# Decay before the second query tile, recurrence between projections, xb to gd in three rounded passes, and a fill dealt out by TensorE's work

## What is computed

```python
z = rms_norm(x, norm_g) @ w_in      # w_in has 1024 rows; its columns are split into:
# qa ka va fa ga | xb gb | qc kcc vcc ksc vsc kwc vwc gate gc | ud vd gd | mg
y_a = fox_attention(rms_norm(qa), rms_norm(ka), va, fa + b_forget)   # adds a cumsum of log_sigmoid(fa)
y_b = rg_lru(conv4(xb), ...)        # two sigmoid gates, tanh/sqrt, a scan over the tokens
y_c = nsa_attention(rms_norm(qc), kcc, ..., vwc, sigmoid(gate))      # compressed + selected + window
y_d = gelu(ud) * (w_spatial @ layer_norm(gelu(vd)) + b_spatial)
ys = stack([y_a * silu(ga), y_b * silu(gb), y_c * silu(gc), y_d * silu(gd)])
merged = sum_n sigmoid(mg_n) * (ys_n @ w_branch_n)
x1 = x + merged @ w_out
```

## Time and profile before

| what | value |
| --- | --- |
| median of 3 runs | 1110.33 us (1109.07 to 1110.61) |
| the profiled execution, own time | 1109.99 us |
| span of its instructions | 1108.2 us |
| TensorE busy | 1005.1 us (91%) |
| VectorE busy | 611.6 us (55%) |
| ScalarE busy | 428.4 us (39%) |
| mean granted TensorE clock | 0.95 |

### The profile page before, as it was taken

How to read it: one execution, slowest core, us unless ns; L and a number is a source line. 1 busy time by engine, 2 the same in 40 slices (tenths; PEclk the granted TensorE clock), 3 DMA queues, 4 the chain that set the end, 5 groups by cost and what they waited for, 6 DMA issues and landing times.

```text
span 1108.2 us, 13860 instructions
## 1 busy us (share of the span) xinstructions
PE 1005.1 (91%) x5638; PEld 762.2 (69%) x5638; DVE 611.6 (55%) x1065; ACT 428.4 (39%) x699; POOL 48.2 (4%) x66
## 2 busy tenths in 40 slices
PE   7979999679997999989879999996889999999984
PEld 5767778446687989849867886896775753566521
DVE  4776521767364464416565599574852621587605
ACT  3345441283465363214365200435651400466401
POOL 1000000000000000000010123000000000000010
PEclk9989999799999999999989999998899999999986
DMA  9725776463424393356143124200898997999993
GB/s 301 227 82 189 262 267 227 152 228 134 171 77 166 111 351 129 116 183 204 36 143 110 44 76 152 77 1 34 323 354 294 352 377 287 399 405 405 408 349 125
DMA packets 110413, 230.66 MB, mean 208 GB/s; under 512 B 8300, under 2 KB 15757, under 8 KB 110350
## 3 DMA queue, kind: packets, MB, share of 16 engines
q1 hardware_dynamic: 104144, 216.44, 54.0%
q0 software_dynamic: 2880, 9.71, 2.3%
q10 hardware_dynamic: 3326, 3.63, 1.1%
HBM read 221.11 MB, written 8.65 MB: 207 GB/s over the span
## 4 chain that ended last, share of the span: by engine, by line
PE 70%; DVE 16%; DMA 6%; ACT 4%; issue 3%; ACTq 0%; DVEq 0%
PE bank L770 10%; PE bank L1510 6%; PE bank L1511 6%; PE bank L1512 6%; PE bank L2573 6%; PE bank L735 5%; PE bank L2512 4%; PE bank L2513 4%; PE bank L2514 4%; PE bank L2597 3%; DMA more_slots<-in_moe_w_up 2%; PE bank L2505 2%; PE bank L1424 1%; DMA slot<-in_ada_w 1%; PE bank L1553 1%
## 5 line engine op out<-in xcount | busy, mean ns | idle before, releaser
L1510 PE MATMUL bank<-rounded 128*128 128x256 f32 (+1 forms) x656 | 201.4, 307 | 14.6 <-DVE slot_rounded L659 8.7
L1511 PE MATMUL bank<-rounded 128*128 128x256 f32 x592 | 168.6, 285 | 0.0
L1510 PEld LDWEIGHTS bank<-rounded 128*128 128x128 f32 x656 | 126.4, 193 | 26.0 <-issue 17.0
L1512 PE MATMUL bank<-rounded,slot_rounded 128*128 128x256 f32 x472 | 135.0, 286 | 0.0
L770 PE MATMUL bank<-x_and_h,slot 128*128 128x256 f32 x544 | 127.5, 391 | 4.9 <-ACT x_and_h L574 4.9
L770 PEld LDWEIGHTS bank<-x_and_h,slot 128*128 128x128 f32 x544 | 104.9, 196 | 23.3 <-issue 8.9
L1511 PEld LDWEIGHTS bank<-rounded 128*128 128x128 f32 x592 | 114.5, 193 | 1.2 <-issue 1.0
L1500 DVE TENSOR_TENSOR slot_rounded<-slot,rounded 128x1024 fp32r<-128x1024 f32 (+1 forms) x63 | 67.1, 1086 | 67.7 <-ACT rounded L1494 67.5
L1512 PEld LDWEIGHTS bank<-rounded,slot_rounded 128*128 128x128 f32 x472 | 91.6, 194 | 0.0
L818 ACT ACTIVATE arena<-bank 128x256 f32<-128x256 f32 x56 | 21.5, 384 | 135.3 <-PE bank L770 108.6
L1494 ACT ACTIVATE rounded<-slot 128x1024 fp32r<-128x1024 f32 (+1 forms) x63 | 57.7, 943 | 27.1 <-PE bank L1512 23.3
(11 more groups left out here) (491 smaller groups left out, 2027.3 us busy)
## 6 DMA issues: line engine op xcount, KB each, us to landing
slot<-in_w_in SPq DMA_DIRECT2D x26, 2048.0 KB, 8.0
slot<-in_ada_w SPq DMA_DIRECT2D x12, 2048.0 KB, 8.2
slot<-in_moe_w_down SPq DMA_DIRECT2D x11, 2048.0 KB, 16.1
more_slots<-in_moe_w_gate SPq DMA_DIRECT2D x8, 2048.0 KB, 15.2
more_slots<-in_moe_w_up SPq DMA_DIRECT2D x8, 2048.0 KB, 17.9
slot<-in_moe_w_gate SPq DMA_DIRECT2D x7, 2048.0 KB, 10.0
x_and_h<-in_moe_w_up SPq DMA_DIRECT2D x6, 2048.0 KB, 15.3
more_slots<-in_moe_w_down SPq DMA_DIRECT2D x5, 2048.0 KB, 17.2
```

Of the source, the lines that this page charges most:

```text
L1510: t.do.matmul(dst, w_hi, x_hi, start=start, stop=False)
L1511: t.do.matmul(dst, w_hi, x_lo, start=False, stop=False)
L1512: return t.do.matmul(dst, w_lo, x_hi, start=False, stop=stop)
```

## The change

1. `decay` moves up in `PLAN`, between the two token tiles of qa. For it SyncE loads `sel` and the 8 columns of `w_f` ahead of the third weight (va), and GpSimd makes its three copies before its other constants.
2. xb (its last two of four channel jobs), gc, gb, ud, vd and gd become three-pass jobs: 18 `channels` jobs and 4 `pieces` jobs (which take the place of two `tokens` jobs of vd) join `FIRST_PIECES`, with 24 new homes. Their hidden-state parts come from `h1_split`, which moves up to stand behind the scores of the last fox unit. As before, the high part is made on ScalarE and the low part on VectorE.
3. `early`, `lru` and `spatial` are written in another order: xb first, then gc, gb and ud, with `conv`, `lru_gates` and `lru` one by one between them.
4. `woven(..., two_behind=24)` is replaced by two calls of `balanced`, which deals out the fill so that its work (by the table `WORK`) per attention job is even, once over the fox units and once over the sparse ones.

```diff
+def balanced(main, fill, cost):
+    whole = sum(cost.get(job[0], 0) for job in fill)
+    fill, out, put = deque(fill), [], 0
+    for n, job in enumerate(main):
+        out.append(job)
+        while fill and (put * len(main) < whole * (n + 1) or not cost.get(fill[0][0])):
+            put += cost.get(fill[0][0], 0)
+            out.append(fill.popleft())
+    return out + list(fill)
...
+        FIRST_HOMES += [M0, M1] + [Y3, M0, M1, SQ0] + [SQ1, Y3, SQ0, SQ1] + [Y3, SQ0, V_HOME, Y3] + [SQ0, V_HOME, Y3, SQ0] + [V_HOME, SQ0, M0, V_HOME]
...
+        LATER_FIRST = len(FIRST_PIECES)
+        FIRST_PIECES += [*channels("xb")[2:], *channels("gc"), *channels("gb"), *channels("ud"), *in_pieces("vd"), *channels("gd")]
+        def piece_beside(job):
+            if job in channels("xb", 2):
+                return LATER_FIRST + job[2]
+            p = FIRST_PIECES.index(job) + 2 if job in FIRST_PIECES else len(FIRST_PIECES)
+            return p if p not in (LATER_FIRST, LATER_FIRST + 1) and p < len(FIRST_PIECES) else None
...
-        PLAN = [..., ("first_start",), *tokens("qa"), FIRST_PIECES[0], ("head_norm", "qa"),
+        PLAN = [..., ("first_start",), ("tokens", "qa", 0), ("decay",), ("tokens", "qa", 1), FIRST_PIECES[0], ("head_norm", "qa"),
-                FIRST_PIECES[6], ("decay",), FIRST_PIECES[7], ("cond",), ...
+                FIRST_PIECES[6], FIRST_PIECES[7], ("cond",), ...
...
+        early += [("cmp_hidden", 0), ("cmp_hidden", 1), ("cmp_flip", 0), xs[0], ("cmp_flip", 1), ("cmp_out",), xs[1], ("conv", 0), ("cmp_keys",), xs[2], ("conv", 1),
+                  ("cmp_scores", 0), xs[3], ("conv", 2), ("cmp_scores", 1), ("cmp_turn", 0), gc[0], ("conv", 3), ("cmp_turn", 1)]
+        lru = [gc[1], ("lru_gates", 0, 0), ("lru_gates", 0, 1), ("softplus",), gc[2], ("lru_gates", 0, 2), ("lru_gates", 0, 3), gc[3], ("lru", 0),
+               ("lru_gates", 1, 0), ("lru_gates", 1, 1), gb[0], ("lru", 1), ("lru_gates", 1, 2), ("lru_gates", 1, 3), gb[1], ("lru", 2),
+               gb[2], ("lru", 3), gb[3], ("lru", 4), ud[0], ("lru", 5), ud[1], ("lru", 6)]
+        WORK = {"pieces": 47, "channels": 25, "tokens": 48, "gates": 19, ...}
+        spatial = [*ud[2:], *in_pieces("vd"), ("spatial_norm",), *channels("gd"), *[("spatial", j) for j in range(WT)]]
...
-        PLAN += woven(scored[:last_units], fill, 24)
+        PLAN += balanced(scored[:first_sparse], fill[:begun], WORK) + balanced(scored[first_sparse:last_units], fill[begun:], WORK)
-        PLAN.insert(PLAN.index(("ada", 6)), ("h1_split",))
+        PLAN.insert(PLAN.index(("scores", UNITS[2 * WT - 1])) + 1, ("h1_split",))
...
+        def sync_decay_constants(s):
+            s.do.dma_start(sel, d["sel"]).then_inc(*dma("sel_in"))
+            s.wait_ge(*at("w_f_clear"))
+            s.do.dma_start(w_f[:, :, 0:NH], w_in[:, :, COL["fa"]:COL["fa"] + NH]).then_inc(*dma("w_f_in"))
...
+                if n == 2:
+                    sync_decay_constants(s)
```

More of the change, by code:

```diff
@@ L413, in build @@
         early = [*kv, *qc[0:2], ("keys_norm", 0), qc[2], ("keys_norm", 1), qc[3], ("gates", 0), ("keys", 0), ("gates", 1), ("head_norm", "qc"),
[L414 to L419, removed]
+                 ("keys", 1), ("cmp_in", 0), ("heads", "qc", 0), ("heads", "qc", 1), ("cmp_in", 1), ("cmp_blocks",)]
+        xs, gc, gb, ud = channels("xb"), channels("gc"), channels("gb"), channels("ud")
+        early += [("cmp_hidden", 0), ("cmp_hidden", 1), ("cmp_flip", 0), xs[0], ("cmp_flip", 1), ("cmp_out",), xs[1], ("conv", 0), ("cmp_keys",), xs[2], ("conv", 1),
[3 more added lines that the diff above has]
+               gb[2], ("lru", 3), gb[3], ("lru", 4), ud[0], ("lru", 5), ud[1], ("lru", 6)]
+        WORK = {"pieces": 47, "channels": 25, "tokens": 48, "gates": 19, "keys": 6, "cmp_in": 36, "heads": 12, "cmp_hidden": 36, "cmp_flip": 3,
+                "cmp_out": 7, "cmp_keys": 2, "cmp_scores": 19, "cmp_turn": 6, "lru_gates": 7, "ada": 22, "ada_turn": 8, "spatial": 12, "merge": 36}
+        spatial = [*ud[2:], *in_pieces("vd"), ("spatial_norm",), *channels("gd"), *[("spatial", j) for j in range(WT)]]
         ada = [job for c in range(13) for job in ((("ada", c),) if c < 12 else ()) + ((("ada_turn", c - 1),) if c else ())]
@@ L464, in build @@
                      "cmp_hidden": (("cmp_k_w1", "cmp_v_w1")[job[-1]],) if job[0] == "cmp_hidden" else ()}.get(job[0], ())
-            for name in names:
+            for name in (*names, *([FIRST_PIECES[piece_beside(job)][1]] if piece_beside(job) else [])):
                 FIRST_USE.setdefault(name, n)
@@ L515, in gpsimd_constants @@
             g.do.memset(w_rg, 0.0).then_inc(*inc("w_rg_clear"))
+            g.wait_ge(*at("w_f_in"))
+            for c in (32, 64, 96):
+                g.do.tensor_copy(w_f[:, :, c:c + NH], w_f[:, :, 0:NH]).then_inc(*inc("w_f_copied"))
             g.do.memset(qcT, 0.0).then_inc(*inc("qcT_clear"))
@@ L521, in gpsimd_constants @@
             g.do.memset(cmp_h, 0.0).then_inc(*inc("cmp_h_clear"))
-            g.wait_ge(*at("w_f_in"))
-            for c in (32, 64, 96):
-                g.do.tensor_copy(w_f[:, :, c:c + NH], w_f[:, :, 0:NH]).then_inc(*inc("w_f_copied"))
         def vector_constants(v):
@@ L681, in tensor_pieces @@
                     k = 2 * j + kk
-                    mm = three_passes(t, bank[:, :], first_high_of_h1[:, k, x], first_low_of_h1[:, k, x], high[:, kk, :], low[:, kk, :], k == 0, k == KT - 1)
+                    mm = three_passes(t, bank[:, :], h_high[:, k, x], h_low[:, k, x], high[:, kk, :], low[:, kk, :], k == 0, k == KT - 1)
             mm.then_inc(*inc("pieces", name, j))
```

76 lines of the change are left out of this document (49 added, 27 removed), and 2 rows, old and new, of the table WEIGHTS.

## The result

The changed kernel takes **1099.82 us** (median of 4 runs, 1098.52 to 1102.34), the kernel before beside it 1110.47 us; the ratio is 0.9916, with a 95% interval of 0.9899 to 0.9934. The change makes the kernel 10.65 us faster. The prediction was 1081 us, range 1069 to 1096: the sign was right, the size was not, and the time lies outside the range.

The account below looks back on a forecast made before the run. TensorE ends last almost everywhere, so a gain must shorten its work or close its gaps. Gains of 6.7 + 13.2 + 9.3 = 29.2 us from 1109.99 us gave 1081 us, range 1069 to 1096 for 8 in 10.

Parts of the forecast that it names:

- moved work: Three attention steps move from ahead of the merges to among them: 1.5 us of TensorE's work, total unchanged.
- Decay early: Ahead of the first fox scores: VectorE's decay steps run where it was idle, the 7.6 us wait goes; 6.7 us gained.
- Three passes: 18 channels jobs and vd get shorter on TensorE: 13.2 us saved; high and low parts free where engines have room.
- (d): At gb 3: ScalarE's 12 table loads and other steps, 31.7 us against TensorE's 29.3; a wait of 4.5 us.
- (a): First sparse mix: VectorE's 31 us up to the second cmp_turned copy against TensorE's 25 us; a wait of 6 us.
- The spreading: Recurrence spread out, 81 to 314 us: 27.3 us of idle time and slow products won, 18 of new waits; 9.3 gained.
- (b): At cmp_hidden 0: VectorE's blocks come behind its copy of ada row 2, head norm and h1 split; about 2.4 us.
- (c): xb's load into the slot ada 2 frees, with the table switches ahead of cmp_out: a wait of 3 us.
- (e): Slower clock behind the new waits: 2 us, estimated as the cost of one slow ada job.
- the in-order engines become the bound: Rival, chance 0.24: 22 new parts on VectorE and ScalarE each 0.5 us late lose 11 us; 1092 us, 1087 to 1106.
- a longer stretch there: Sign of being wrong: the stretch behind the first merge longer than its earlier 794.5 us, which nothing in the working explains.
- above 0.9: Sign of being right: TensorE's granted clock above 0.9 in every stretch up to the first merge.

Follow-up runs that it names:

- decay alone: The kernel before with only the decay, its load, its mask's load and its copies moved between the two qa tiles: 1105.17 us, ratio 0.9956.
- new order with plain products: The changed kernel in its new order, but xb 2 to gd as plain one-pass products and vd as two token tiles: 1092.38 us, ratio 0.9848.
- The filled waits: The changed kernel with 37 extra products on TensorE ahead of four waits (cmp_hidden 0, first sparse mix, gb 3, gd 2): 1088.52 us, ratio 0.9804.
- norm later: The changed kernel with VectorE's norm of vd behind gd 1 instead of ahead of gd 0: 1092.38 us, ratio 0.9846.

## Why the prediction was wrong

Term by term, in the profiled executions: the early decay 3.8 us ahead of the scores (6.7 predicted), the new order 18.0 us between scores and merge (9.3 and 1.5 of moved work), the three passes 7.3 us **lost** there (13.2 gained), and 5.1 us lost behind the first merge (1.5).

**Decay early: 6.7 us predicted, 3.9 measured.** (ga 3 ending at 74.3 for 80.8 would be 6.5.) The new waits for low parts (4.5 us predicted, 4.6 measured) were right. Behind the wait that went I had counted slow products as saved; behind the wait of 2.6 us that took its place there are slow products again (in "decay alone" the mean granted clock is 0.88 from 46 to 60 us, before it was 1.00).

**Three passes: 13.2 us of work saved, parts that "cost nothing only where those engines have room".** The work saved was near enough: 11.4 us, by two kernels in whose TensorE jobs nothing else differs (the norm of vd and the split of h1 stand elsewhere in the other engines' orders). The step that failed is the other half: the price of the 22 parts, which the sum put at nothing in this term. TensorE was made to wait directly for only three of them between scores and merge (8.6 us in sum) and it stood longer at the first sparse mix, where four more stand in VectorE's way; that was enough: taking the three passes back takes 11 us of idle time out of this stretch and makes the kernel 7.4 us faster. The waits (d), at gb 3, and part of (a), four low parts of 1.2 us each, were costs of the three passes, which I had booked under the spreading; and the largest, gd 2's 5.5 us, I had not looked for. I had followed ScalarE and VectorE job by job up to gb 3 and stopped there, where ScalarE's table loads end. The norm of vd, 8 us of VectorE in one go further on, had hurt nothing in the kernel before, where no part had to pass it.

**The spreading: 27.3 - 18 = 9.3 us.** From the decay alone to the new order with plain products the stretch between scores and merge shrinks from 232.3 to 214.3 us, 18 us, of which 1.5 are the moved attention work; by the medians it is 12.8 us. So the new order gave more than I had booked for it, in part because some of the waits that I had taken off were the three passes'.

**(a) to (e), one by one.** (a) 4.7 us for 6, right in kind. (b) 4.6 for 2.4: right place; of the steps named for it the split of h1, with VectorE's 2.1 us of standing for its high part, was the one that mattered, and not the copy of ada 2. (c) 1.0 us at `cmp_out` and 0.6 for weights, for 3. (d) 2.5 for 4.5 (its own terms, 31.7 - 29.3 + 0.4 + 1.2, make 4.0). The table loads are there as counted. One of them on ScalarE in the changed kernel, between an activation that ends at 222.28 + 1.06 and the next:

```profile
222.28 1.06 ACT L1388 ACTIVATE arena<-arena 128x1024 f32<-128x1024 f32 x1
223.36 1.28 ACT L1376 ACT_TABLE_LOAD   x1
224.66 0.84 ACT L1376 ACTIVATE arena<-bank,par 128x256 f32<-128x256 f32 x2
```

A switch costs 1.3 us here, as in the earlier trace rows. By the 2.66 us of the Trainium skill (ScalarE: Activation LUTs, What ACT_TABLE_LOAD costs) this wait would have been some 16 us longer than predicted (an estimate, 12 x 1.36); it was shorter, and the row decides.

(e) is the wrongly sized one among these: **2 us for the clock, where about 8 were paid in four places.** Behind the four waits `cmp_hidden 0` took 6.4 us for 3.6, gc 1 4.9 for 2.9, gb 3 4.5 for 2.9 and gd 2 4.6 for 3.0, 8.0 us in sum, and the slow short jobs came on top. I had the idle time nearly right (20.3 us in all, where 16 of new waits were predicted) and had seen slow products in the old profile, but took them as a mark of the thin middle of the kernel, which the change would fill, and not as a price that a new wait can bring with it. The filled waits show that it can: 8.9 us in this stretch.

**Which rival it was.** The second, "the in-order engines become the bound", had the right mechanism, late parts, but looked for many small waits where there were few and large ones. The measured time lies in its range (1087 to 1106), 8 us above its 1092; it had no price for the clock either. Its 48 us for ScalarE stand in no row: the earlier trace rows add up to 104.6, and in the changed kernel ScalarE is busy 131.7 of 221.4 us.

**Behind the first merge** the changed kernel lost 5.1 us, of which 1.5 us are the moved attention work; the prediction had named a longer stretch there as a sign of being wrong. The kernels with this same order there range from 793.1 to 800.9 us from merge to end. It is not idle time that differs, but how long TensorE's work takes, as these rows of the kernels before, changed and with the norm later show:

```profile
312.47:1108.20 795.73, 728.56 (x4092) 555.33 (x4090) 441.27 (x692) 294.23 (x445) 42.08 (x52) 0.95 0.57 210
298.40:1099.30 800.90, 735.90 (x4106) 560.80 (x4104) 443.42 (x697) 296.08 (x449) 42.06 (x52) 0.95 0.56 209
292.00:1087.60 795.60, 730.03 (x4107) 555.89 (x4104) 444.11 (x700) 298.53 (x453) 42.00 (x52) 0.96 0.56 209
```

TensorE is idle 67.2, 65.0 and 65.6 us there; for the same jobs it is busy 735.9 us in the changed kernel and 730.0 with the norm later, at a mean granted clock of 0.95 and 0.96. So the clock has a part in these differences too; why it is granted for longer in one kernel than in another was not tried.

**As predicted** came out: no wait at the decay product, the convolution and low parts ahead of the first sparse mix with VectorE busy, the channels jobs as 24 products of 0.12 us, no stall on xb's load, and the wait of ka 3 (2.6 us for 3). The clock did not stay above 0.9 as foretold: from 136 to 197 us it was 0.87.

## What to carry to other kernels

A new wait of several us on TensorE can cost its length plus slow work behind it: here 1.6 to 2.8 us more behind four waits of 2.5 to 5.5 us, and nothing behind one of 3.1 us, so the sum needs both bounds. Work taken from TensorE and given to two in-order engines is a gain only where the new instructions have no long step ahead of them on either: follow each one through both queues to the end of the stretch, and look first for the longest single step in their way. A wait that stays when its supposed cause is moved away has mostly another cause: read the timeline of the engine that it names, from the wait backward, before moving anything.

## What was not expected of the hardware

A kernel that does 37 products more is 1.0% faster. And the length of a wait alone does not say whether the work behind it is slow: behind the wait at gb 3, 2.5 us, the next job took 4.5 us instead of 2.9, while behind the wait of 3.1 us that was left at the first sparse mix when `cmp_turn 1` went ahead, gc 1 took its usual 2.9. What decides between the two was not tried.
